# First feed-forward of a two-block transformer kernel: twelve pairs of up-projection chunks as seven half-width block products, squared row norm moved to the down products

## The reference, cut to what matters

```python
h = rms_norm(x, norm2_g)                         # x * r * g, r = 1/sqrt(mean(x^2) + eps) of a token
f = jnp.square(jax.nn.relu(h @ w_ff1))           # 512 x 4096
x = x + f @ w_ff2
```

## Time and profile before

| | us |
|---|---|
| median of three runs | 1158.57 |
| the profiled execution's own time | 1156.93 |
| its span | 1154.9 |
| PE busy (share of the span) | 1139.6 (99%) |
| DVE, ACT, POOL busy | 597.4, 288.1, 711.4 |

### The profile page before, as it was taken

One profiled execution on the slowest core, in us unless ns is written; L12 is line 12 of the kernel. 1 busy time (PEld: TensorE's weight loads), 2 busy tenths in 40 slices (PEclk: granted clock), 3 DMA queues, 4 the chain that ended last, 5 costly groups with the idle time before them and its releaser, 6 DMA issues.

```text
span 1154.9 us, 15364 instructions
## 1 busy us (share of the span) xinstructions
PE 1139.6 (99%) x5307; PEld 921.6 (80%) x5307; DVE 597.4 (52%) x988; ACT 288.1 (25%) x577; POOL 711.4 (62%) x435
## 2 busy tenths in 40 slices
PE   7999999999999999999999999999999999999997
PEld 6888788888888888888778777777888888888886
DVE  4999674540014544457789777847554000545022
ACT  5134352210002211111202356546421000111001
POOL 7879948666656666666556333225876666656662
PEclk9999999999999999999999999999999999999999
DMA  6321214223223223224342222012332232223621
GB/s 251 121 92 55 79 67 146 91 99 101 91 96 105 91 92 109 91 91 147 110 128 92 89 81 65 26 54 74 95 122 92 91 104 97 91 97 103 146 73 74
DMA packets 51394, 113.12 MB, mean 98 GB/s; under 512 B 21520, under 2 KB 22160, under 8 KB 51344
## 3 DMA queue, kind: packets, MB, share of 16 engines
q1 hardware_dynamic: 31200, 105.40, 27.2%
q10 hardware_dynamic: 20144, 7.05, 2.6%
HBM read 102.99 MB, written 2.10 MB: 91 GB/s over the span
## 4 chain that ended last, share of the span: by engine, by line
PE 92%; DVE 6%; ACT 1%; issue 1%; DMA 0%; DVEq 0%; SPq 0%; ACTq 0%
PE bank L569 21%; PE bank L570 20%; PE bank L571 20%; PE bank L1110 5%; PE bank L1111 5%; PE bank L1112 5%; DVE bank L1618 2%; PE bank L955 2%; PE bank L603 1%; PE bank L601 1%; PE bank L602 1%; PE bank L635 1%; PE bank L627 1%; PE bank L628 1%; PE bank L969 1%
## 5 line engine op out<-in xcount | busy, mean ns | idle before, releaser
L434 POOL TENSOR_TENSOR wl<-raw,wh 128x1024 fp32r<-128x1024 f32 x188 | 452.8, 2409 | 15.7
L431 POOL TENSOR_SCALAR wh<-raw 128x1024 fp32r<-128x1024 f32 x188 | 202.8, 1079 | 385.4 <-PE bank L571 227.7
L569 PE MATMUL bank<-xh,wh 128*128 128x512 f32 (+1 forms) x776 | 306.1, 394 | 0.0
L571 PE MATMUL bank<-xh,wl 128*128 128x512 f32 (+1 forms) x776 | 300.8, 388 | 0.0
L570 PE MATMUL bank<-xl,wh 128*128 128x512 f32 (+1 forms) x776 | 300.7, 388 | 0.0
L569 PEld LDWEIGHTS bank<-xh,wh 128*128 128x128 f32 x776 | 145.7, 188 | 44.0 <-issue 16.2
L1833 DVE TENSOR_TENSOR ul<-tmb,uh 128x512 f32 x64 | 124.7, 1949 | 90.0 <-ACT uh L1286 90.0
L571 PEld LDWEIGHTS bank<-xh,wl 128*128 128x128 f32 x776 | 145.7, 188 | 29.6
L570 PEld LDWEIGHTS bank<-xl,wh 128*128 128x128 f32 x776 | 145.8, 188 | 27.5 <-issue 0.2
L1285 ACT ACTIVATE tmb<-tmp 128x512 f32<-128x512 f32 x64 | 40.5, 632 | 413.3 <-DVE tmp L1830 413.3
L569 PE MATMUL bank<-uh,wh 128*128 128x512 f32 x288 | 112.7, 391 | 0.0
(11 more groups left out here) (282 smaller groups left out, 1378.0 us busy)
## 6 DMA issues: line engine op xcount, KB each, us to landing
raw<-wstream SPq DMA_DIRECT2D x188, 512.0 KB, 3.2
x<-xT SPq DMA_DIRECT2D x8, 256.0 KB, 4.5
x4r<-x4b ACTq DMA_DIRECT2D x16, 128.0 KB, 2.6
out<-x4r SPq DMA_DIRECT2D x8, 256.0 KB, 2.3
qd<-ropey ACTq DMA_DIRECT2D x16, 64.0 KB, 2.1
kd<-ropey ACTq DMA_DIRECT2D x16, 64.0 KB, 2.0
qa<-ropey SPq DMA_DIRECT2D x16, 64.0 KB, 2.0
ka<-ropey SPq DMA_DIRECT2D x16, 64.0 KB, 2.0
```

The costliest lines, as they stand in the source:

```text
L431: nc.gpsimd.tensor_scalar(wh[c][:], raw[c][:], 1.0, 1.0, ALU.mult, ALU.mult).then_inc(high_ready, 1)
L434: nc.gpsimd.tensor_tensor(wl[c][:], raw[c][:], wh[c][:].bitcast(F32), ALU.subtract).then_inc(split_ready, 1)
L569: mm(out, wh_, mh, start=start, stop=False)
L571: return mm(out, wl_, mh, start=False, stop=stop)
```

## The change

The first eight up chunks stay as they are (`PLAIN` is 8; four of them in `feed_first`, four in `feed_forward`). The other 24 become twelve pairs: four in the first half (p 0 to 3), eight in the second (p 4 to 11). A pair is a product of a 2 x 2 block matrix of weights (two chunks of output rows, each in two halves of the contraction) and a 2 x 2 block matrix of `x` (contraction in two halves, tokens in two halves `EARLY` and `LATE`). It is done in seven block products in place of eight. A block product (`product`) is four contraction steps of three matmuls with 256 columns.

Four sums of blocks of gained x are needed as moving operands, `t_high` and `t_low`. They are made once, in four groups (`t_sums`, `scaled_parts`, `t_round`), by DVE and ACT after plain chunks 1, 2, 4 and 5 (`T_AFTER`). Four sums of weight blocks are made for each pair on DVE from `raw` (`weight_sums_first`, `weight_sums_last`), rounded by ACT (`sum_round`) and given their low part by DVE (`weight_rest`), one pair ahead. POOL splits only the three blocks that are used as they are (`split_pair`). The products' sums are put together on DVE (`first_corner` to `fourth_product`), ACT keeps the first product, and makes relu and squares (`raise_tile`, `square_tile`). The factor r no longer goes into `tmp`: `rb` is squared once (`link(mul(rb, rb, rb))`), and each of the 16 down tiles is multiplied by it (`scaled_down`). Four small DVE operations for the lambda of the second block (`lam_products`, before at L1867 to L1870 at the end of the first feed-forward) move ahead of the first up chunk, and the load of the cosine and sine tables moves behind the second half's up chunks.

```diff
+PLAIN = 8
+T_AFTER = (1, 2, 4, 5)
...
+def pair_runs():
+    return ((0, PLAIN), (FH // 2 - PLAIN // 2, 2 * FH))
+def pairs_of(h):
+    first, at = pair_runs()[h]
+    last = (FH // 2 - PLAIN // 2) if h == 0 else first + FH // 2
+    return range(first, last)
...
+for h in range(2):
+    first, last = chunk_of(pairs_of(h)[0]), chunk_of(pairs_of(h)[-1]) + 2
+    for n in range(first + SLOTS, last + SLOTS):
+        sp.wait_ge(sum_made, 4 * (pairs_of(h)[0] + (n - SLOTS - first) // 2 + 1))
+        load(n)
...
+def split_pair(p):
+    if alone:
+        pool.wait_ge(chunk_done, n - 3)
+    else:
+        pool.wait_ge(product_done, 6 * (p - 1) + 2)
+    nc.gpsimd.tensor_scalar(wh[0][:], a[:], 1.0, 1.0, ALU.mult, ALU.mult).then_inc(high_ready, 1)
+    pool.wait_ge(high_ready, n + 1)
+    nc.gpsimd.tensor_tensor(wl[0][:, 0:512], a[:, 0:512], wh[0][:, 0:512].bitcast(F32), ALU.subtract)
+    nc.gpsimd.tensor_tensor(wl[0][:, 512:], a[:, 512:], wh[0][:, 512:].bitcast(F32), ALU.subtract
+                            ).then_inc(split_ready, 1)
+    pool.wait_ge(raw_loaded[(n + 1) % SLOTS], 16 * ((n + 1) // SLOTS + 1))
+    pool.wait_ge(chunk_done, n)
...
+def product(out, slot, part, mh, ml):
+    for k in range(4):
+        ks = slice(512 * part + k * P, 512 * part + k * P + P)
+        last = three(out, wh[slot][:, ks], wl[slot][:, ks], mh(k), ml(k), k == 0, k == 3)
+    return last
+def pair(p, e, alone):
...
+    pe.wait_ge(split_ready, n + 1)
+    if alone:
+        pe.wait_ge(evacuated, e - 3)
+    else:
+        pe.wait_ge(part_added, 5 * p - 3)
+    product(out[0], 0, 0, lambda k: xh[:, k, EARLY], lambda k: xl[:, k, EARLY]).then_inc(product_done, 1)
+    if alone:
+        pe.wait_ge(evacuated, e - 2)
+    else:
+        pe.wait_ge(part_added, 5 * p - 2)
+    product(out[1], 0, 1, lambda k: xh[:, 4 + k, EARLY], lambda k: xl[:, 4 + k, EARLY]
+            ).then_inc(product_done, 1)
+    if p == 0:
+        pe.wait_ge(t_ready, 16)
+    pe.wait_ge(sum_ready, 4 * p + 1)
+    if alone:
+        pe.wait_ge(evacuated, e - 1)
+    else:
+        pe.wait_ge(part_added, 5 * p)
+    product(out[2], 1, 1, lambda k: t_high[1][:, k], lambda k: t_low[1][:, k]).then_inc(product_done, 1)
+    pe.wait_ge(sum_ready, 4 * p + 2)
+    pe.wait_ge(evacuated, e if alone else e - 1)
+    product(out[3], 1, 0, lambda k: t_high[0][:, k], lambda k: t_low[0][:, k]).then_inc(product_done, 1)
+    pe.wait_ge(sum_ready, 4 * p + 3)
+    pe.wait_ge(evacuated, e)
+    if alone and p:
+        pe.wait_ge(down_out, 8)
+    product(out[4], 2, 0, lambda k: t_high[2][:, k], lambda k: t_low[2][:, k]).then_inc(product_done, 1)
+    pe.wait_ge(sum_ready, 4 * p + 4)
+    pe.wait_ge(product_kept, p + 1)
+    product(out[5], 2, 1, lambda k: xh[:, 4 + k, LATE], lambda k: xl[:, 4 + k, LATE]
+            ).then_inc(product_done, 1)
+    pe.wait_ge(split_ready, n + 2)
+    pe.wait_ge(part_added, 5 * p + 1)
+    product(out[6], 3, 0, lambda k: t_high[3][:, k], lambda k: t_low[3][:, k]).then_inc(chunk_done, 2)
     for h in range(2):
         up0 = c0 + 2 * FH * h
-        with pe.Fori(1 - h, FH // 4) as r:
-            for c in range(4):
-                pe.wait_ge(split_ready, r * 4 + (up0 + c + 1))
-                pe.wait_ge(evacuated, r * 4 + (e0 + h * FH + c - 3))
-                chunk_transposed((up0 + c) % SLOTS, bank[c][:], xh, xl)
+        if h == 0:
+            for c in range(4, PLAIN):
+                pe.wait_ge(split_ready, up0 + c + 1)
+                pe.wait_ge(evacuated, e0 + c - 3)
+                chunk_transposed((up0 + c) % SLOTS, bank[c % 4][:], xh, xl)
+        for p in pairs_of(h):
...
+def scaled_parts(k):
+    act.wait_ge(t_ready, 4 * k)
+    A(bank[4][:, EARLY], x[:, k, EARLY], ACT.Copy, scale=col("norm2", k)).then_inc(scaled_part, 1)
+    A(bank[5][:, EARLY], x[:, 4 + k, LATE], ACT.Copy, scale=col("norm2", 4 + k)).then_inc(scaled_part, 1)
+def t_round(k):
+    for i, (t, src) in enumerate(((0, bank[4][:, EARLY]), (2, bank[5][:, EARLY]),
+                                  (1, bank[4][:, LATE]), (3, bank[5][:, LATE]))):
+        act.wait_ge(t_made, 4 * k + (2 if i < 2 else i + 1))
+        A(t_high[t][:, k], src, ACT.Copy).then_inc(t_rounded, 1)
...
+def sum_round(p, i):
+    n = chunk_of(p)
+    alone = p == pairs_of(0 if n < C_FF1 + FH else 1)[0]
+    slot, part, made = ((1, 1, 2), (1, 0, 1), (2, 0, 4), (2, 1, 3))[i]
+    act.wait_ge(sum_made, 4 * p + made)
+    if alone:
+        act.wait_ge(chunk_done, n - 3 + slot)
+    else:
+        act.wait_ge(product_done, 6 * (p - 1) + 3 + i)
+    A(wh[slot][:, 512 * part:512 * part + 512], bank[7 - made % 2][:], ACT.Copy).then_inc(sum_rounded, 1)
+def keep_product(p):
+    first = pairs_of(0 if p < FH // 2 - PLAIN // 2 else 1)[0]
+    act.wait_ge(product_done, 6 * p + 1)
+    if p > first:
+        act.wait_ge(part_added, 5 * p - 3)
+    A(first_product[:], bank[7 * (p - first) % 5][:, EARLY], ACT.Copy).then_inc(product_kept, 1)
+def raise_tile(p, i):
+    f = tile_pair(p) + i
+    act.wait_ge(evacuated, E_FF1 + f + 1)
+    A(pair_buffer(p, i), pair_buffer(p, i), ACT.Relu).then_inc(raised, 1)
+    act.wait_ge(raised, 2 * p + i + 1)
+    A(uh[:, f % FH], pair_buffer(p, i), ACT.Square).then_inc(uh_ready, 1)
...
+def square_tile(p, i):
+    f = tile_pair(p) + i
+    act.wait_ge(ul_ready, f)
+    A(bank[5][:], pair_buffer(p, i), ACT.Square).then_inc(square_ready, 1)
+for c in range(PLAIN):
+    act.wait_ge(evacuated, E_FF1 + c + 1)
+    A(uh[:, c], sq[c % 2][:], ACT.Square).then_inc(uh_ready, 1)
+    A(sq[c % 2][:], sq[c % 2][:], ACT.Square).then_inc(square_ready, 1)
+    if c in T_AFTER:
+        scaled_parts(T_AFTER.index(c))
+        t_round(T_AFTER.index(c))
+    if c == PLAIN - 2:
+        for i in range(4):
+            sum_round(0, i)
+for h in range(2):
+    run = pairs_of(h)
+    if h:
+        for i in range(4):
+            sum_round(run[0], i)
+        act.wait_ge(down_out, 8)
+    for p in run:
+        keep_product(p)
+        if p > run[0]:
+            square_tile(p - 1, 1)
+        if p < run[-1]:
+            for i in range(4):
+                sum_round(p + 1, i)
+        raise_tile(p, 0)
+        square_tile(p, 0)
+        raise_tile(p, 1)
+    square_tile(run[-1], 1)
+act.wait_ge(chunk_done, C_FF1 + 3 * FH)
 act.dma_start(cosr[:], a["cos"]).then_inc(tables_loaded, 16)
 act.dma_start(sinr[:], a["sin"]).then_inc(tables_loaded, 16)
...
+def t_sums(k):
...
+    def scaled_less(out, src, gain, other):
+        V.scalar_tensor_tensor(out=out, in0=src, scalar=gain, in1=other, op0=ALU.mult, op1=ALU.subtract
+                               ).then_inc(t_made, 1)
+    def t_rest(t, src, rounded):
+        dve.wait_ge(t_rounded, 4 * k + rounded)
+        V.tensor_tensor(t_low[t][:, k], src, t_high[t][:, k].bitcast(F32), ALU.subtract
+                        ).then_inc(t_ready, 1)
+    dve.wait_ge(scaled_part, 2 * k + 2)
+    scaled_less(t1, first[:, LATE], g1, t1)
+    scaled_less(t3, first[:, LATE], g1, t3)
+    dve.wait_ge(t_made, 4 * k + 2)
+    t_rest(0, t1, 1)
+    scaled_less(t2, second[:, LATE], g2, t1)
+    t_rest(2, t3, 2)
+    dve.wait_ge(t_made, 4 * k + 3)
+    t_rest(1, t2, 3)
+    scaled_less(t4, second[:, EARLY], g2, t2)
+    dve.wait_ge(t_made, 4 * k + 4)
+    t_rest(3, t4, 4)
+def weight_sums_first(p):
...
+        dve.wait_ge(sum_ready, 4 * p)
+    V.tensor_tensor(bank[6][:], rbw[:, 0:512], rbw[:, 512:], ALU.add).then_inc(sum_made, 1)
+    dve.wait_ge(sum_made, 4 * p + 1)
+    V.tensor_tensor(bank[7][:], bank[6][:], ra[:, 0:512], ALU.subtract).then_inc(sum_made, 1)
+def weight_sums_last(p):
+    ra, rbw = raws(p)
+    dve.wait_ge(sum_ready, 4 * p + 2)
+    V.tensor_tensor(bank[6][:], ra[:, 512:], bank[7][:], ALU.subtract).then_inc(sum_made, 1)
+    V.tensor_tensor(bank[7][:], bank[7][:], rbw[:, 512:], ALU.subtract).then_inc(sum_made, 1)
+def weight_rest(p, i):
+    slot, part, made = ((1, 1, 2), (1, 0, 1), (2, 0, 4), (2, 1, 3))[i]
+    at = slice(512 * part, 512 * part + 512)
+    dve.wait_ge(sum_made, 4 * p + made)
+    dve.wait_ge(sum_rounded, 4 * p + i + 1)
+    V.tensor_tensor(wl[slot][:, at], bank[7 - made % 2][:], wh[slot][:, at].bitcast(F32), ALU.subtract
+                    ).then_inc(sum_ready, 1)
...
+def first_corner(p):
+    dve.wait_ge(product_done, 6 * p + 2)
+    dve.wait_ge(product_kept, p + 1)
+    V.tensor_tensor(pair_buffer(p, 0)[:, EARLY], product_bank(p, 1), first_product[:], ALU.add
+                    ).then_inc(part_added, 1)
+def second_product(p):
+    dve.wait_ge(product_done, 6 * p + 3)
+    V.tensor_tensor(second_sum[:], product_bank(p, 2), first_product[:], ALU.add).then_inc(part_added, 1)
...
+def third_product(p):
+    dve.wait_ge(product_done, 6 * p + 6)
+    dve.wait_ge(part_added, 5 * p + 5)
+    out = pair_buffer(p, 0)[:, LATE]
+    V.tensor_tensor(out, product_bank(p, 5), out, ALU.add).then_inc(evacuated, 1)
...
+def rest_of_tile(f, src):
+    dve.wait_ge(square_ready, f + 1)
```

(55 more changed lines are left out.)

130 lines of the change are left out of this document (109 added, 21 removed).

## The result

| | before | after |
|---|---|---|
| median, us | 1158.59 (1157.15 to 1158.93, four runs) | 1171.45 (1170.47 to 1172.61, four runs) |
| profiled execution, its span | 1156.93, 1154.9 | 1172.25, 1170.5 |

The ratio is 1.0116, 95% interval 1.0104 to 1.0127: 13 us slower. The single executions of the changed kernel lie between 1170.47 and 1172.61, so a median of four can't settle a difference of 1 or 2 us. I had forecast 1176 in 1163 to 1186, and slower with 0.87.

A forecast was written before the change was run, and what follows sets the result against it. PE bounds the kernel, busy 1139.6 of 1154.9 us. Pairs -6.4, preparation +21.9, clock +2.0 and the rest 0 make +17.5 on 1158.57, so 1176, in 1163 to 1186; slower with 0.87.

The forecast's parts named there:

- rival D: DVE operations that meet POOL don't wait, the rest as forecast: 4.8 us less, 1171; counted within the forecast's 0.76.
- 256 columns at 0.120 apart: PE's pair products: 84 matmuls at 0.120 take 10.08 us against 10.88 for two plain chunks, 9.6 gained for twelve.
- The 20 us: Twelve pairs' gain on PE by the skill's matmul rule, a pair taking 9.2 us, if nothing else bound them.
- The pair's loop: DVE and ACT between pairs: a 10.7 us loop, first pairs at PE's 10.08, 10.35 taken for all, gain 6.4 us.
- Meetings with POOL: At the list's start, DVE operations with two SBUF inputs wait for POOL: first max at 185.1, 182.4 if none waits.
- The list: DVE's serial work before pair 0 delays PE's third product to 226.3 and the fourth to 231.1, costing 21.9 us.
- The clock: PE's wait of 10 us lowers its clock; two products, some 22 matmuls, run slow, costing 2.0 us, bounds 0 and 4.
- The rest: Multiplying down tiles, second-half weight sums, weight transfers and POOL's split: cost 0, at most 0.8 us for the last down tile.
- B: Pairs slower than two chunks, 11.3 to 11.6 us each, the twelve losing 5 to 9: 1190; chance 0.11.
- A: Preparation hidden, third product's operands there by 207.8, only pairs count: about 1151; chance 0.08.
- C: Preparation costs only what pairs give back, all low ends at once, clock never falls: 1159; chance 0.05.

The follow-up runs named there:

- group_early8: As `all_later8`, with chunk 7's max ahead of pair 0's last two weight sums and the first group of sums ahead of the norm's total: 1150.18 us.
- factor_psum: Changed kernel with lambda products ahead of the norm's total, rb's squaring behind the first pairs, second squares of plain chunks 0 to 5 in PSUM: 1165.51 us.
- one_group: Changed kernel with three of the four groups of sums of x left out, all products reading the first group's: 1157.20 us.
- rest_later: Changed kernel with each plain chunk's low part issued one chunk later and ACT's scaled halves ahead of the chunk's squares: 1162.04 us.
- square_only: Kernel before with only the squared norm factor multiplied onto the down products, no pairs and no sums: 1158.74 us, ratio 1.0006.
- second_half: Changed kernel with all 16 first-half chunks plain, eight pairs only in the second half, groups of sums behind chunks 3, 6, 9, 12: 1155.72 us.
- warm_again: Changed kernel with extra 256-column matmuls in PE's waits of pair 0, 18 behind the first product and 80 behind the second: 1171.42 us.
- all_later8: Changed kernel with lambda products and rb's squaring moved away, low parts one chunk later, plain chunks' second squares in PSUM: 1156.52 us.

## Why the prediction was right, and where its terms were off

The case was right: the pairs save PE time, and the preparation in front of them costs more. The number came out 4.6 us high (1176 against 1171.45). It is also just what rival D gave (1171), but that is chance: D's mechanism is not there, as the meetings did wait, and the difference comes from the pairs. By steps:

- **256 columns at 0.120 apart:** 0.119. Right; the rule of the Trainium skill ("TensorE: Matmul & The Clock Gate", Back-to-back issue gap: 109 ns) is not what the trace shows, at 512 columns (0.2267) or at 256. That section calls the rule the gap of an isolated matmul, and its figure for a stream of weight loads and matmuls, 131 ns at 512 columns, is not what the trace shows either. The 20 us in the prediction also took a pair by the rule from two chunks as measured; with the rule on both sides, an estimate from the same section, it is 12 x (48 x 0.216 - 84 x 0.109) = 14.5.
- **The pair's loop, gain 6.4 us:** measured 8.8 (3.2 + 5.6). Of the terms this one was off most. I had the loop at 10.7 us; it is 10.46. The last three sixth products of the second run, which need ACT's keep:

```profile
412.61 0.36 PE L670 MATMUL bank<-xh,wh 128*128 128x256 f32 x1
423.07 0.36 PE L670 MATMUL bank<-xh,wh 128*128 128x256 f32 x1 [0.17 <-ACT first_product L1468]
...
433.54 0.35 PE L670 MATMUL bank<-xh,wh 128*128 128x256 f32 x1 [0.15 <-ACT first_product L1468]
```

  They are 10.46 apart, so the last two of the eight pairs go at the loop's rate. The first five go at PE's, (405.35 - 355.01) / 5 = 10.07, and the mean is 10.18. The slack at the start of the run lasts for about six pairs. I had written that only the first pairs go at PE's rate, and then took half of the difference for all twelve without working out the slack. ACT's keeps show how it is used up:

```profile
356.71 0.39 ACT L1468 ACTIVATE first_product<-bank 128x256 f32<-128x256 f32 x1 [5.13 <-DVE x L2189]
...
412.10 0.36 ACT L1468 ACTIVATE first_product<-bank 128x256 f32<-128x256 f32 x1
422.56 0.37 ACT L1468 ACTIVATE first_product<-bank 128x256 f32<-128x256 f32 x1
433.03 0.36 ACT L1468 ACTIVATE first_product<-bank 128x256 f32<-128x256 f32 x1
```

  Seven intervals in 76.32 us are 10.9 each. Four are 10.46 to 10.48; the other three are 11.35 to 11.67, and in them DVE's first weight sum, with its two SBUF inputs, lasts 1.39 to 1.67 us beside POOL and not 0.69. In `group_early8` the loop is reached in the first run already: its pairs of the first half are the 10.5 us above.
- **Meetings with POOL:** right where I put them, 2.31 and 1.18 us; first max forecast for 185.1, measured 185.08. `factor_psum` shows the mechanism.
- **The list, third product at 226.3, fourth at 231.1:** 225.69 and 230.29. From the first max (185.08) to the third product it is 40.6 us against 41.2: 19.3 for the seven plain chunks (forecast 20.7), 4 x 4.59 = 18.4 for the groups (17.6), 2.95 for the weight sums (2.9). Two small errors partly cancel. By the prediction's own numbers the third product is 226.3 - 207.8 = 18.5 late, not 18.7, and the fourth 3.4 more, not 3.2; the total of 21.9 is right. Of the pieces, chunk 7 had been put at 2 us and is 0.23. That the list is on the path is shown: `one_group`, `rest_later` and `factor_psum` each take out another part of it, and PE follows.
- **The clock, 2.0 us:** 1.7. But PE ran slow in more places than I said: at chunk 4 (0.427 for 512 columns), in the second product, the third and the fourth. What comes before the fourth product is covered, so the term came out near because DVE's list hid the rest. In part this is luck.
- **The rest at 0:** right, by `square_only`.

Sum by these terms: 17.9 + 3.2 + 1.7 - 8.8 = 14.0, forecast 17.5. Of the 3.5 us between, 2.4 are the pairs, 0.8 the preparation and 0.3 the clock. Of the rivals, B (pairs slower) falls by the pairs' 10.07 to 10.46 us and by `second_half`. A needed the third product's operands at 207.8, 17.9 earlier than they came; `group_early8` brings them there (208.21), and its 1150.18 is about the 1151 that A gave. C needed a preparation of 10 us, and it cost 21.1.

## What to carry to other kernels

When work moves from the bounding engine to one at half load, write down the helper's list from its first operation to the first result that the bounding engine needs, with its waits for third engines, and compare two clock times; the busy share says nothing about it. Then do the same for the loop that follows: a run goes at the bounding engine's pace only while its starting slack lasts (six pairs of eight here). Then look for what of the list can go ahead of its start, behind a later item, or into the helper's idle stretch: here such moves alone turned 13 us lost into 7 us won with the same arithmetic. And before an experiment shortens one wait, ask which wait is next behind it; warming PE for a product whose bank comes late anyway gave nothing.

## What the runs showed of the hardware that I had not expected

- The clock fell behind short waits, but not behind each. After 2.65 us of idle PE, matmuls of 512 columns were 0.427 apart from the second on, for 3.7 us. After 2.36 us at 213.88, all twelve of 256 columns were 0.213 apart. After the wait of 2.93 us in `warm_again`, the matmuls were slow for over 5 us, although PE had hardly paused from 214.17 to 227.6. In the same trace PE idles 2.65 us before chunk 4 as in the changed kernel, and there the clock stays full (0.23 apart from 186.49 on). In `rest_later` a wait of 2.70 us leaves it full too, and it falls 0.6 us after the next wait, of 2.93; in `all_later8` it falls 1.4 us after a wait of the same length. So the length of one wait doesn't decide it, and what does is open.
- POOL held a DVE operation of 64 elements for 2.31 us, as long as one of 512 (2.45). And the place decides: moved 5.9 us earlier, the same list met other POOL operations and lost 2.4 us of the move.
